# Convolution module: LayerNorm, swish and the product behind it in two halves of 256 tokens, with the sums of the mean moved among the last taps

## The reference, cut to what matters

```python
def conformer_conv(h, pw1_w, pw1_b, dw_w, dw_b, ln_g, ln_b, pw2_w, pw2_b):
    a = h @ pw1_w + pw1_b
    u, gate = jnp.split(a, 2, axis=-1)
    u = u * jax.nn.sigmoid(gate)
    y = lax.conv_general_dilated(u, dw_w[:, None, :], ...) + dw_b   # causal, 31 taps, per channel
    y = layernorm(y, ln_g, ln_b)       # mean and variance over the 1024 channels of a token
    y = jax.nn.silu(y)
    return y @ pw2_w + pw2_b

def reference(x, ...):
    for i in range(2):                 # mixer 0: the convolution above, mixer 1: attention
        x = x + rmsnorm(mixer_i(rmsnorm(x)))
        x = x + rmsnorm(squared_relu_mlp(rmsnorm(x)))
    return x
```

## Time and profile before

| | us |
|---|---|
| median of 3 runs | 1168.86 (1166.03 to 1168.88) |
| the profiled execution, its own time | 1168.7 |
| its span, from first to last instruction | 1167.0 |
| TensorE busy | 1143.3 (98%) |
| VectorE busy | 903.2 (77%) |
| ScalarE busy | 660.0 (57%) |
| GpSimd busy | 195.0 (17%) |
| mean granted TensorE clock | 0.998 |

### The profile page before, as it was taken

One profiled execution on the slowest core, in us unless ns is written; L12 is line 12 of the kernel. 1 busy time (PEld: TensorE's weight loads), 2 busy tenths in 40 slices (PEclk: granted clock), 3 DMA queues, 4 the chain that ended last, 5 costly groups with the idle time before them and its releaser, 6 DMA issues. The chain is left out here.

```text
span 1167.0 us, 16099 instructions
## 1 busy us (share of the span) xinstructions
PE 1143.3 (98%) x5608; PEld 960.3 (82%) x5608; DVE 903.2 (77%) x1356; ACT 660.0 (57%) x1113; POOL 195.0 (17%) x181
## 2 busy tenths in 40 slices
PE   7999999999999999999899999999999999999997
PEld 6888888988888888887888888888888888888886
DVE  5899965689479578589898888884797588586698
ACT  5778866565444353445687666665566354343453
POOL 4588840210000000003420001000300000000003
PEclk9999999999999999999999999999999999999999
DMA  5422122421521513312222222222423414315301
GB/s 151 109 72 72 37 75 68 150 72 37 181 72 50 174 66 122 131 37 55 55 55 55 75 69 72 72 73 73 144 72 101 147 42 143 110 37 181 108 19 73
DMA packets 103675, 102.30 MB, mean 88 GB/s; under 512 B 4621, under 2 KB 86541, under 8 KB 103610
## 3 DMA queue, kind: packets, MB, share of 16 engines
q1 hardware_dynamic: 103532, 101.29, 27.3%
q10 hardware_dynamic: 78, 0.16, 0.1%
HBM read 99.34 MB, written 2.10 MB: 87 GB/s over the span
## 5 line engine op out<-in xcount | busy, mean ns | idle before, releaser
L643 PE MATMUL psum<-hhi,whi 128*128 128x512 f32 x792 | 313.5, 396 | 0.5 <-DVE tmp L1976 0.3
L645 PE MATMUL psum<-hhi,wlo 128*128 128x512 f32 x792 | 309.5, 391 | 0.0
L644 PE MATMUL psum<-hlo,whi 128*128 128x512 f32 x792 | 309.2, 390 | 0.0
L1194 ACT ACTIVATE whi<-mraw 128x1024 fp32r<-128x1024 f32 x176 | 185.5, 1055 | 143.0 <-PE psum L920 113.6
L1716 DVE TENSOR_TENSOR wlo<-mraw,whi 128x1024 fp32r<-128x1024 f32 x176 | 214.3, 1223 | 42.3 <-ACT whi L1194 42.3
L918 PE MATMUL psum<-whi,aop_hi 128*128 128x512 f32 x448 | 175.1, 391 | 0.8 <-DVE wlo L1716 0.8
L645 PEld LDWEIGHTS psum<-hhi,wlo 128*128 128x128 f32 x792 | 149.1, 188 | 31.9
L643 PEld LDWEIGHTS psum<-hhi,whi 128*128 128x128 f32 x792 | 149.4, 189 | 30.7 <-issue 1.5
L920 PE MATMUL psum<-whi,aop_lo 128*128 128x512 f32 x448 | 174.4, 389 | 0.0
L919 PE MATMUL psum<-wlo,aop_hi 128*128 128x512 f32 x448 | 174.4, 389 | 0.0
L644 PEld LDWEIGHTS psum<-hlo,whi 128*128 128x128 f32 x792 | 149.4, 189 | 29.2
(11 more groups left out here) (259 smaller groups left out, 1974.0 us busy)
## 6 DMA issues: line engine op xcount, KB each, us to landing
mraw<-in_mlp_w_up SPq DMA_DIRECT2D x64, 512.0 KB, 5.0
mraw<-in_mlp_w_down SPq DMA_DIRECT2D x64, 512.0 KB, 4.5
wraw<-in_conv_pw_w SPq DMA_DIRECT2D x20, 512.0 KB, 4.5
wraw<-in_attn_w_in SPq DMA_DIRECT2D x16, 512.0 KB, 5.0
wraw<-in_attn_w_in SPq DMA_DIRECT2D x16, 256.0 KB, 3.1
wraw<-in_attn_w_o SPq DMA_DIRECT2D x8, 512.0 KB, 4.6
xin<-in_x SPq DMA_DIRECT2D x4, 512.0 KB, 6.9
wraw<-in_conv_pw_w SPq DMA_DIRECT2D x8, 256.0 KB, 6.7
```

What stands on the lines that cost most here:

```text
L643: pe.matmul(o, whi[:, u, kb, :], xhi, start=start, stop=False)
L644: pe.matmul(o, whi[:, u, kb, :], xlo, start=False, stop=False)
L645: return pe.matmul(o, wlo[:, u, kb, :], xhi, start=False, stop=stop)
L1194: a.activation(split_unit(whi, e), raw_unit(c, e_), ACT.Copy).then_inc(s["m_hi"], 1)
```

## The change

- The dummies: `WARM_ROOT` 5 to 3, `WARM_NORM` 13 to 8, `WARM_TAPS` 4 to 2, `WARM_SUB` 10 to 3, and one instead of three between the columns.
- End of the convolution: POOL does `y_total` of block 6 ahead of the four `tap_sums` of block 7 instead of behind them. TensorE's sums of `sumsq` and block 6 move from behind the last block's taps to between its 12 extra and its 7 usual ones. `join` of block 7 goes to a psum bank, so that L1870 adds psum and `y`. ACT splits units 2, 3, 0, 1, and DVE splits the rest of units 2 and 3 between `join` and L1870, where it was behind the squares before.
- LayerNorm: the subtraction goes over tokens 0 to 255 for all blocks, then over tokens 256 to 511 (three blocks ahead of the inverse, two behind it, three among the norms). ACT squares the first half. POOL squares the second half (`c_late`). TensorE sums both by one-column matmuls block by block, with no pairing before: the first half's before its root, the second half's (32 records) behind block 4 of the first half's product.
- Root, inverse, spread, norm, Silu, `hhi`, `hlo` once for each half, with tables fetched in the order Sqrt, Silu, Sqrt, Silu (each a load and a one-element activation) and then Sqrt as before.
- The product: `first_step` (96 matmuls of 512 columns) becomes 96 of 256 columns over the first half, the spread of the second half's inverse, and 96 of 256 columns over the second. The last two blocks of the second half go unit by unit, as before.

The diff, with three hunks (names of semaphores and of the two norms, a branch in `root`) and blank lines left out:

```diff
@@ -29,7 +29,7 @@
 LOOP_TAPS = 3
 MORE_TAPS = 4 * LOOP_TAPS
 POOL_SUMS = POOL_TAPS - 1
-WARM_SQ, WARM_ROOT, WARM_NORM, WARM_TAPS, WARM_SUB, WARM_START = 4, 5, 13, 4, 10, 2
+WARM_SQ, WARM_ROOT, WARM_NORM, WARM_TAPS, WARM_SUB, WARM_START = 4, 3, 8, 2, 3, 2
 MASK = 1e30
 RMS_EPS = 1e-6
 LN_EPS = 1e-5
...
@@ -500,12 +501,12 @@
                 g.tensor_tensor(ulo[:, r, :], upad[:, r, :], uhi[:, r, :].bitcast(F32),
                                 ALU.subtract).then_inc(s["u_ready"], 1)
-            def tap_sums(j, ks=range(1, POOL_TAPS)):
+            def tap_sums(j, ks=range(1, POOL_TAPS), behind=0):
                 for k in ks:
                     pool.wait_ge(s["tap_act"], ACT_TAPS * j + (3 + k))
                     if k > 1:
-                        pool.wait_ge(s["y_sum"], y_sums(j) + (k - 1))
+                        pool.wait_ge(s["y_sum"], y_sums(j) + (k - 1 + behind))
                     g.tensor_tensor(blk(y, j), blk(y, j), prods[:, k - 1, :], ALU.add).then_inc(s["y_sum"], 1)
             def conv_lo(n, u):
@@ -514,13 +515,14 @@
                 g.tensor_tensor(wlo[:, u, :, :], wraw[:, u // 2, :, c * P:(c + 1) * P],
                                 whi[:, u, :, :].bitcast(F32), ALU.subtract).then_inc(w_ready[u // 2], 1)
-            def y_total(j, r, add=True):
-                at_ = y_sums(j + 1) + POOL_SUMS
+            def y_total(j, r, last=False):
+                at_ = y_sums(j + 1) + (0 if last else POOL_SUMS)
                 pool.wait_ge(s["y_done"], j + 1)
                 pool.wait_ge(s["y_sum"], at_)
                 g.tensor_tensor(blk(y, j), blk(y, j), acc1[:, r, :], ALU.add).then_inc(s["y_sum"], 1)
-                if not add:
+                if last:
                     return
                 pool.wait_ge(s["y_sum"], at_ + 1)
                 g.tensor_tensor(sumsq[:, :], sumsq[:, :], blk(y, j), ALU.add).then_inc(s["y_sum"], 1)
@@ -562,16 +564,13 @@
             u_lo(KB - 1, 1)
             tap_sums(KB - 2, range(3, POOL_TAPS))
             y_total(KB - 3, 1)
-            tap_sums(KB - 1)
-            y_total(KB - 2, 0, add=False)
+            y_total(KB - 2, 0, last=True)
+            tap_sums(KB - 1, behind=1)
             for u in (0, 1):
                 conv_lo(N_PW2, u)
-            pool.wait_ge(s["c_sq"], 4)
-            g.tensor_tensor(sumsq[:, :], m[:, 1, :], m[:, 3, :], ALU.add).then_inc(s["c_add"], 1)
-            pool.wait_ge(s["c_add"], 1)
-            pool.wait_ge(s["c_sq"], 6)
-            g.tensor_tensor(sumsq[:, :], sumsq[:, :], m[:, 5, :], ALU.add).then_inc(s["c_add"], 1)
+            for k in range(KB):
+                pool.wait_ge(s["c_sub"], KB + k + 1)
+                g.tensor_tensor(m[:, k, LATE], y[:, k, LATE], y[:, k, LATE], ALU.mult).then_inc(s["c_late"], 1)
             add_squares(1)
@@ -829,6 +828,9 @@
                 for k in range(more):
                     one(W - PE_TAPS - more + k, morehi[:, k, :], morelo[:, k, :], k == 0, False)
                 if more:
+                    pe.wait_ge(s["y_sum"], y_sums(KB - 1) + 1)
+                    pe.matmul(psum[:, STAT, :], ones[:, :], sumsq[:, :], start=True, stop=False)
+                    pe.matmul(psum[:, STAT, :], ones[:, :], y[:, KB - 2, :], start=False, stop=False)
                     pe.wait_ge(s["diag"], KB - 1)
                 for k in range(PE_TAPS):
                     mm = one(W - PE_TAPS + k, diaghi[:, r, k, :], diaglo[:, r, k, :], k == 0 and not more,
@@ -867,28 +869,46 @@
                     conv(2 * i + (r - 1), 1 - r)
             conv(KB - 1, 1, MORE_TAPS)
-            pe.wait_ge(s["y_sum"], y_sums(KB) - 1)
-            pe.matmul(psum[:, STAT, :], ones[:, :], sumsq[:, :], start=True, stop=False)
-            pe.matmul(psum[:, STAT, :], ones[:, :], y[:, KB - 2, :], start=False, stop=False)
             keep_warm(WARM_TAPS)
             pe.wait_ge(s["y_done"], KB)
             pe.matmul(psum[:, STAT, :], ones[:, :], y[:, KB - 1, :], start=False,
                       stop=True).then_inc(s["mean"], 1)
             keep_warm(WARM_SUB, 0)
-            for k in (0, 2, 4):
+            for k in range(KB):
                 pe.wait_ge(s["c_sq"], k + 1)
-                columns(m[:, k, :], k == 0, False, 7)
-                keep_warm(3, 0)
-            pe.wait_ge(s["c_pair"], 1)
-            columns(m[:, 7, :], False, False, 7)
-            pe.wait_ge(s["c_add"], 2)
-            columns(sumsq, False, True, 7).then_inc(s["c_sum"], 1)
+                mm = token_columns(OUTP, 0, m[:, k, :], (0, 1), k == 0, k == KB - 1)
+                if k < KB - 1:
+                    keep_warm(1, 0)
+            mm.then_inc(s["c_sum"], 1)
             keep_warm(WARM_ROOT, 0)
-            broadcast(NTH[ST_VAR])
+            pe.wait_ge(s["irms_done"], NTH[ST_VAR[0]])
+            token_spread(4, 0, (0, 1)).then_inc(s["bcast"], 1)
             keep_warm(WARM_NORM, 0)
-            first_step(N_PW2, s["c_ready"], 0)
+            def second_conv(h, ks, units):
+                for u in units:
+                    for kb in ks:
+                        pe.wait_ge(s["c_ready"], KB * h + kb + 1)
+                        mm = part_product(u, u, kb, hhi, hlo, (EARLY, LATE)[h], h == 0 and kb == 0,
+                                          h == 1 and kb == KB - 1)
+                return mm
+            for u in range(4):
+                weights(N_PW2, u)
+            for kb in range(KB):
+                second_conv(0, (kb,), range(4))
+                if kb == 4:
+                    for k in range(KB):
+                        pe.wait_ge(s["c_late"], k + 1)
+                        mm = token_columns(STAT, 0, m[:, k, :], (2, 3), k == 0, k == KB - 1)
+                    mm.then_inc(s["c_sum"], 1)
+            pe.wait_ge(s["irms_done"], NTH[ST_VAR[1]])
+            token_spread(5, 0, (2, 3)).then_inc(s["bcast"], 1)
+            for kb in range(KB - 2):
+                second_conv(1, (kb,), range(4))
+            for u in range(4):
+                second_conv(1, (KB - 2, KB - 1), (u,)).then_inc(unit[u // 2], 1)
             for u in range(2):
                 pe.wait_ge(s["m_done"], u + 3)
                 whole_unit(N_PW2 + 1, u)
...
@@ -1362,22 +1379,39 @@
             first_taps(KB - 1, 1)
             next_diagonals(KB - 2, 0)
             pool_taps(KB - 1, 1)
-            for u in range(4):
+            for u in (2, 3, 0, 1):
                 split_hi(N_PW2, u)
             fetch_table(1, ACT.Sqrt)
             for k in range(KB):
                 act.wait_ge(s["c_sub"], k + 1)
-                a.activation(m[:, k, :], y[:, k, :], ACT.Square).then_inc(s["c_sq"], 1)
-            root(ST_VAR, 1, 7)
-            for k in range(KB):
-                act.wait_ge(s["c_nrm"], k + 1)
-                if k >= 2:
-                    act.wait_ge(s["c_ready"], k - 1)
-                a.activation(tmp[:, k % 2, :], y[:, k, :], ACT.Silu, scale=vcol(V_LNG, k),
-                             bias=vcol(V_LNB, k)).then_inc(s["c_silu"], 1)
-                act.wait_ge(s["c_silu"], k + 1)
-                a.activation(hhi[:, k, :], tmp[:, k % 2, :], ACT.Copy).then_inc(s["c_hi"], 1)
+                a.activation(m[:, k, EARLY], y[:, k, EARLY], ACT.Square).then_inc(s["c_sq"], 1)
+            def conv_root(h):
+                tiles = (slice(0, 2), slice(2, 4))[h]
+                act.wait_ge(s["c_sum"], h + 1)
+                a.activation(rms[:, tiles], psum[:, (OUTP, STAT)[h], tiles], ACT.Sqrt, scale=1.0 / D,
+                             bias=eps[:, 1:2]).then_inc(s["root"], 1)
+            def conv_silu(h):
+                rows = (EARLY, LATE)[h]
+                for k in range(KB):
+                    n = KB * h + k
+                    act.wait_ge(s["c_nrm"], n + 1)
+                    if n >= 2:
+                        act.wait_ge(s["c_ready"], n - 1)
+                    a.activation(tmp[:, k % 2, rows], y[:, k, rows], ACT.Silu, scale=vcol(V_LNG, k),
+                                 bias=vcol(V_LNB, k)).then_inc(s["c_silu"], 1)
+                    act.wait_ge(s["c_silu"], n + 1)
+                    a.activation(hhi[:, k, rows], tmp[:, k % 2, rows], ACT.Copy).then_inc(s["c_hi"], 1)
+            conv_root(0)
+            fetch_table(5, ACT.Silu)
+            conv_silu(0)
+            fetch_table(6, ACT.Sqrt)
+            conv_root(1)
+            fetch_table(7, ACT.Silu)
+            conv_silu(1)
             def mixer_out(n0, b, dst, bias_row, row_pre):
@@ -1864,32 +1898,59 @@
             finish(KB - 2, 0)
             for i in range(DVE_TAPS - MORE_TAPS):
                 tap(KB - 1, 1, i, DVE_TAPS - MORE_TAPS)
-            join(KB - 1, 1, MORE_TAPS)
+            dve.wait_ge(s["tap"], DVE_TAPS * KB - MORE_TAPS)
+            d.tensor_tensor(psum[:, 0, :], psum[:, 0, :], acc1[:, 1, :], ALU.add).then_inc(s["acc"], 1)
+            for u in (2, 3):
+                split_lo(N_PW2, u)
             dve.wait_ge(s["acc"], KB)
-            dve.wait_ge(s["y_sum"], y_sums(KB - 1) + POOL_SUMS)
```

(61 more changed lines are left out.)

## The result

The changed kernel takes 1176.83 us (median of 4 runs, 1175.77 to 1177.36) against 1168.82 before. The medians are 8.0 us apart; the ratio by which the runs are compared is 1.0062 (95% interval 1.0046 to 1.0078), 0.62% slower. The profiled execution took 1175.77 us, 7.1 more than that of before.

The account below looks back on a forecast made before the run. TensorE was taken as the bound, so its start of the second four units decides: +0.55 - 4.95 - 0.4 + 7.45 + 1.75 = +4.4 us onto 1168.7, giving 1173.1 us, range 1168.5 to 1177.0.

Parts of the forecast that it names:

- a clock row below 1.00 in between: Sign in the profile after: a lowered granted clock inside the stretch makes the prediction wrong by the price given.
- its leading case: The main sum up to the second four units: +4.4 us, 1173.1 us; chance 0.42.
- the case of the clock: Rival: TensorE's clock falls once more, about 3.3 us at the lower level, costing 1.7; +6.1, 1174.8 us; chance 0.20.
- The mean: End of convolution to first subtraction: DVE and POOL hold each other, taps end later; +0.55 us, bounds -0.55 and +0.55.
- the rival: DVE and POOL don't hold each other; POOL's taps end by 152.5, `hlo` isn't held; +2.9, 1171.6 us; chance 0.22.
- To the first norm: First subtraction to first norm: 7.4 us at full clock instead of 12.35, 4.95 gained, about 1.9 of it the old low clock.
- To the first product: First norm to first product: shorter passes gain 2.1; table load adds 0.15, `hlo` beside POOL's squares 0.4; 0.4 us gained.
- The product and the next weights: First product to second four units: product with columns and uncovered spread loses 7.45 us, waiting for `wlo` 1.75.
- The free columns: Rival: one-column records are nearly free or hide under products, both trains (7.2 us) go; -2.8, 1165.9 us; chance 0.10.
- The drain at a table load: Rival from the skill's page: a table switch drains ACT, first Silu 1.4 us later; +5.8, 1174.5 us; chance 0.03.

Follow-up runs that it names:

- e5_port: Changed kernel with DVE's two weight subtractions (units 2 and 3) put back behind the mean's subtractions; ran once for its profile, no ratio; first subtraction 0.5 us earlier.
- e4_warm: Changed kernel with two dummy matmuls instead of one between the first half's columns, 14 records more; 1.0071 of the kernel before.
- e6_mean: Kernel before with only the end of the convolution changed, norm and product whole, DVE's weight subtractions in their old place; 0.998 of the kernel before.
- e8_pooladd: Changed kernel with spread behind block 5, last four blocks unit by unit, two dummies between columns, POOL adding second-half squares (4 records for 32); 1.0004 of before.
- e2_tail: Changed kernel with the last four blocks of the second half's product going unit by unit instead of the last two; 1.0071 of the kernel before.
- e10_dense: Halves with earlier spread, last four blocks unit by unit, POOL-summed and DVE-paired squares, 15 dummies ahead of the columns, none between; 1165.2 us, 0.9972 of before.

## Why the prediction was right or wrong

The direction, the holes and the range (1168.5 to 1177.0) held, the range with 0.2 us to spare; the forecast of +4.4 us was 3.6 short of the measured +8.0. By the prediction's own signs (a clock row below 1.00 in between) its leading case, at 0.42, did not come. What came is the case of the clock, at 0.20, with two falls in place of one. Step by step, before to changed kernel, from the table:

- *The mean*, forecast +0.55, measured -0.05. The two engines do hold each other, as the forecast had it and the rival hadn't, but POOL's taps lost 1.6 us, not 2.3: the last two came 2.26 apart, not 2.6, and the pair cost POOL less than its own length. e5_port gives the price at A alone, 0.5.
- *To the first norm*, forecast -4.95 "at full clock", measured -2.03. This is the step that failed most. The rate of 0.112 a record was right: e4_warm, with 14 records (1.57 us) more and no fall, needs 9.09, so the changed list needs 7.5 at full clock, where 7.4 were forecast. But the clock fell, 6.8 us in both profiles of the changed kernel, and took 2.8 in the first. In the second it took 1.7 here and 0.5 behind the norm, where the eight slowed dummies took 3.50 and the product stood behind them. The prediction's 1.9 for the end of the old fall was somewhat high as well: e6_mean gives 1.6. The forecast counted the end of the old fall as a gain and put the new one among the rivals, though it made TensorE's work between 154 and 165 sparser than before: a wait of 0.9, dummies cut from 10 to 3 and from three to one.
- *To the first product*, forecast -0.4, measured -0.54. The 0.4 for `hlo` beside POOL's squares is there (0.85 instead of 0.43, see e8_pooladd).
- *The product and the next weights*, forecast +9.2, measured +10.78. Every price held: P to R in e8_pooladd is 23.99, which is 192 matmuls of 0.120 and 0.95 for columns and spread; the columns 3.6; the hole with its spread 185.32 to 187.98, 2.66, forecast 2.74; the wait for `wlo`, 1.75 by e2_tail. What is left, about 1.6, is the second fall of the clock; e2_tail, without it, has 1.5 less.
- *The rivals.* The clock's rival had the mechanism and the price of one fall of 3.3 us (1.7). Two came, and 4.4 + 1.7 + 1.7 = 7.8 is near the result, but that is partly luck: the first fall was twice as long and cost 2.8, the second 1.6, and the mean came 0.6 cheaper than forecast. The free columns are refuted by e8_pooladd (3.10 for 28 records). The drain at a table load, 1.4 us more by its rival, is refuted here. At the first root the load starts 0.29 behind the root's start, and ACT later waits 1.02 us for the norm, so the load isn't on the path. At the second root of the changed kernel the load starts 0.28 behind it, and the next instruction when the load ends:

```profile
179.62 0.26 ACT L1393 ACTIVATE rms<-psum,eps 128x2 f32<-128x2 f32 x1 [3.38 <-PE psum L703]
179.90 1.28 ACT L1247 ACT_TABLE_LOAD   x1
181.19 0.20 ACT L1247 ACTIVATE unused<-eps 128x1 f32<-128x1 f32 x1
```

What stays open: which of the sparse places brings a fall in a given execution. With one dummy between the first half's columns it fell there in 6 of 6 profiles, with two, or with pairs, in 0 of 5. With the list of the kernel before, which has three, it fell in one of two (before, but not e6_mean). From P to R, with the train of 32 records or the hole or both, it fell in 6 of 7 profiles, and without them in 0 of 4. e2_tail, the seventh, had both and no fall. So sparse work makes a fall much likelier here; it does not settle whether and when one comes, and 13 profiles of single executions can't tell the share of each place.

## What to carry to other kernels

Where TensorE is the bound, a split in halves has to be paid on its own list: count every extra record at the weight load's pace, and look for the chain of the other engines that nothing covers, behind the last instruction in front of the second half. Put what starts that chain (here the spread) two blocks earlier and let the last blocks finish unit by unit, so that the next weights have their cover again. Taking dummies away can change the clock: e4_warm put 14 records in and was 1.2 us shorter from A to P. Dummies ahead of the columns, where TensorE would wait anyhow, cost nothing here, and dummies between them did: e10_dense moved six records from between to ahead, won 0.7, and the clock stayed up. Price a fall in the main sum whenever an edit makes a stretch sparser.

## What was not expected of the hardware

The one kernel before varied from 1165.55 to 1172.54 us over the runs of these comparisons. The slowest go with a lower mean granted clock, 0.993 or 0.994 at 1171.12 to 1172.54, but the clock doesn't tell all: 0.998 stands beside 1165.55 and beside 1170.54. A second place for falls lies around 580 us, where TensorE waits 1.51 us at the first product of layer 1 (timeline of the kernel before, whose profile has the wait and no fall):

```profile
578.32 0.39 PE L1016 MATMUL psum<-hhi,wfhi 128*128 128x256 f32 x1 [1.51 <-DVE hlo L2199]
```

Of the 13 profiles four have no fall there, two have 3.4 us of low clock, seven 6.8. The part behind R takes 972.7 to 973.6 us in the four, 974.5 and 975.0 in the two, 974.9 to 977.2 in the seven. From R up to that place the thirteen agree within 0.15 us. So a profile's span alone could not have told e2_tail's gain from nothing; the parts of the stretch could. And up to TensorE's last matmul every fall in these profiles lasted 3.4 or 6.8 us, wherever it was.
